# GpSimd's low-part subtractions of the expert weights, one instruction of 1024 columns against four of 256

## The chip, the cores and the metric

The kernel is one program on one core of a Trainium2 chip. The metric is the device time of one execution in microseconds (us). A core has a TensorE for matmuls (PE; PEld is its weight load), a VectorE (DVE), a ScalarE (ACT), a GpSimd (POOL), a SyncE (SP) that issues transfers, and 16 DMA engines. Each engine works through its own list of instructions in order and meets the others only at semaphores.

## The reference

It is one layer of a hybrid streaming encoder over 1024 prompt frames and 64 frames of a running stream, 1088 tokens of width 1024. After a mixer (band attention and retention) comes the part that the change touches, a retrieval over 16384 experts of one neuron each:

```python
qry = (hb @ w_query).reshape(t, P_HEADS, 2, P_HALF)
...
expert = jnp.take_along_axis(cand_i, best_pos, axis=-1)      # 8 heads x 16 experts a token
gate = jax.nn.softmax(best_s, axis=-1)
a = jnp.einsum('td,thkd->thk', hb, expert_u[expert]).astype(jnp.float32)
act = (jax.nn.gelu(a, approximate=False) * gate).astype(hb.dtype)
return jnp.einsum('thk,thkd->td', act, expert_v[expert])
```

Everything is in fp32. A matmul of fp32 precision is made of three passes over numbers split into a high part (rounded to fp32r) and a low part (the rest): high times high, high times low, low times high.

## The kernel before, in words

The program runs five stages one after the other: projection, mixer (`mix_...`), routing, spreading of the gates, and the experts (`exp_...`), which begin near 1900 us and take the second half of the time. The expert stage does its work in two ways at once.

**The dense way**, for the last 704 tokens: all 16384 experts are computed, 128 at a time, in 128 steps j. Step j needs `u_raw` and `v_raw` of j (128x1024 each, a transfer of 512 KB each, from SP), split in two parts. ScalarE copies them to fp32r (`u_hi`, `v_hi`), GpSimd subtracts that from the raw values (`u_lo`, `v_lo`, line 1587 and line 1592). TensorE multiplies `u` with the hidden state (`up`, L1800), ScalarE applies gelu (`ge`), VectorE multiplies by the gates (`pr`, L1703), ScalarE rounds it (`am_hi`), VectorE subtracts (`am_lo`, L1708), TensorE multiplies with `v` (`vp`, L1813), and VectorE adds the result from PSUM to `acc` (L1715). A step has 96 matmuls of 352 columns.

**The gathered way**, for the first 384 tokens: each of the 128 experts of a token is fetched by its index. A fetch is an indirect DMA that GpSimd issues (L1601): it brings one row of 1024 for each of 128 tokens into one of four slots of `ring`. VectorE then does a "pick" over the slot: in the first half of the stage a multiply with reduction into `dot` (L1722, followed by a short read of the accumulator), in the second half a multiply-add into `own` (L1728). There are 768 fetches and 768 picks, 12 in a pair of steps.

The order on each engine is written out by hand. For each pair of steps, q, VectorE goes through 16 places m: an addition at each, a product (L1703) at m = 0, 4, 8 and 12, an `am_lo` (L1708) at m = 1, 5, 9 and 13, and a pick at 12 of them:

```python
LATE = (3, 4, 6, 7, 8, 9, 10, 11, 12, 13, 14, 15)
SPOTS = (0, 1, 2, 3, 4, 6, 7, 8, 10, 11, 12, 14)
```

GpSimd goes through the same pair as four splits with three fetches behind each: `split_u`, three fetches, `split_v`, three fetches, `split_u`, three fetches, `split_v`, three fetches. Fetch n waits until pick n-4 has left its slot (`after(pool, taken, n - RING + 1)`), pick n waits until fetch n has landed (`row_in`). TensorE alternates blocks of six `up` and six `vp` matmuls; at m = 0 and m = 8 its `vp` part waits for an `am_lo`, and each `vp` block waits until VectorE has emptied one of four PSUM banks (`added`).

Of the kernel before, what the change touches and what calls it, by code (L numbers as in the profile page):

```python
# [8 lines left out]
F32 = mybir.dt.float32  # L9
# [3 lines left out]
ALU = mybir.AluOpType  # L13
# [4 lines left out]
D = 1024  # L18
# [35 lines left out]
def after(eng, sem, value):  # L54

    if not isinstance(value, int) or value > 0:
        eng.wait_ge(sem, value)
# [1427 lines left out]
def experts(nc, d):  # L1485
# [11 lines left out]
    with Stage(nc, "exp") as s:  # L1497
        h2 = [s.sb("h2_hi", [P, KD, TD], F32R), s.sb("h2_lo", [P, KD, TD], F32R)]
        acc = s.sb("acc", [P, KD, TD])
        u_raw = s.sb("u_raw", [P, 2, KD * P])  # L1500
        v_raw = s.sb("v_raw", [P, 2, D])
        u = [s.sb("u_hi", [P, 2, KD * P], F32R), s.sb("u_lo", [P, 2, KD * P], F32R)]
        v = [s.sb("v_hi", [P, 4, D], F32R), s.sb("v_lo", [P, 4, D], F32R)]
# [77 lines left out]

        @block.gpsimd
        def _(pool):

            def split_u(j):
                pool.wait_ge(u_hi_ready, j + 1)
                nc.gpsimd.tensor_tensor(u[1][:, j % 2, :], u_raw[:, j % 2, :], u[0][:, j % 2, :].bitcast(F32),  # L1587
                                        ALU.subtract).then_inc(u_lo_ready, 1)

            def split_v(j):  # L1590
                pool.wait_ge(v_hi_ready, j + 1)
                nc.gpsimd.tensor_tensor(v[1][:, j % 4, :], v_raw[:, j % 2, :], v[0][:, j % 4, :].bitcast(F32),  # L1592
                                        ALU.subtract).then_inc(v_lo_ready, 1)

            def fetch(n):

                if n >= 2 * PICKS:
                    return
                after(pool, taken, n - RING + 1)
                k, t = n % PICKS // NS, n % NS  # L1600
                nc.gpsimd.indirect_dma_start(  # L1601
                    out=ring[:, n % RING, :], out_offset=None, in_=d["u_rows"] if n < PICKS else d["v"],
                    in_offset=bass.IndirectOffsetOnAxis(ap=eid[:, t, k:k + 1], axis=0)).then_inc(row_in[n % RING], 16)

            pool.wait_ge(eid_in, 16)
            for n in range(RING):
                fetch(n)
            split_u(0)
            for q in range(NQ):
                n = EACH * q + RING  # L1610
                split_u(2 * q + 1)
                for s_ in range(0, 3):
                    fetch(n + s_)
                split_v(2 * q)
                for s_ in range(3, 6):
                    fetch(n + s_)
                if q + 1 < NQ:
                    split_u(2 * q + 2)
                for s_ in range(6, 9):
                    fetch(n + s_)  # L1620
                split_v(2 * q + 1)
                for s_ in range(9, EACH):
                    fetch(n + s_)
# [280 lines left out]
```

## Time and profile before

| | |
|---|---|
| median of 3 runs | 4056.29 us (4054.91 to 4061.13) |
| the profiled execution: time / span | 4058.68 us / 4056.7 us |
| PE busy | 3551.1 us, 88% |
| DVE busy | 3035.6 us, 75% |
| POOL busy | 1640.1 us, 40% |
| ACT busy | 1109.6 us, 27% |
| mean granted TensorE clock | 0.955 |

The busy time of an engine is what lies between the starts and the ends of its instructions. An instruction that has started and is held up before it can read its data counts as busy. So the mean duration of a kind of instruction is to be compared with its shortest one.

### The profile page before, as it was taken

The page shows a single profiled execution, that of the slowest core. Times are in us where ns is not written, and L with a number is a line of the kernel's source. Part 1 is how long each engine was busy: PE and PEld are TensorE (multiplying, and loading weights), DVE is VectorE, ACT ScalarE, POOL GpSimd, SP SyncE. Part 2 cuts the span into 40 slices and gives each one's busy share as a digit, 9 for nine tenths or more (in the row PEclk, how much of TensorE's full clock was granted, in tenths as well). Part 3 has the DMA queues.
Part 4 walks back from the last instruction along what each step waited for, and adds up shares of the span by engine and source line. Part 5 has one row for each costly group of instructions (what it writes and reads, how often), then busy time and mean ns, then how long its engine had stood idle before and what let it go on. Part 6 is the DMA issues. An engine that isn't in the chain of part 4 may idle for free.

```text
span 4056.7 us, 55884 instructions
## 1 busy us (share of the span) xinstructions
PE 3551.1 (88%) x20014; PEld 3207.7 (79%) x20014; DVE 3035.6 (75%) x5650; ACT 1109.6 (27%) x1636; POOL 1640.1 (40%) x1154
## 2 busy tenths in 40 slices
PE   7999978999979842663899999999999999999998
PEld 6888865566568732663899999999999999999998
DVE  3110104433337998995999999999999999999998
ACT  3211213333211113994222222222222222222221
POOL 0000013232000000001766666666667777777774
PEclk9999988999989976997999999999999999999999
DMA  3222233222230000557888888888878888888887
GB/s 128 96 94 92 88 137 145 97 85 90 65 131 24 4 7 16 166 166 228 283 275 273 280 274 278 279 276 273 278 262 273 281 283 279 277 281 277 282 281 244
DMA packets 335784, 775.24 MB, mean 191 GB/s; under 512 B 39088, under 2 KB 142512, under 8 KB 334256
## 3 DMA queue, kind: packets, MB, share of 16 engines
q0 software_dynamic: 110592, 402.70, 29.5%
q1 hardware_dynamic: 198160, 336.04, 24.7%
q10 hardware_dynamic: 26912, 35.13, 2.4%
q8 instruction: 46, 0.75, 0.1%
q14 instruction: 74, 0.61, 0.0%
HBM read 680.73 MB, written 93.06 MB: 191 GB/s over the span
## 4 chain that ended last, share of the span: by engine, by line
DVE 37%; issue 9%; PE 5%; DMA 1%; POOL 1%; DVEq 0%; ACTq 0%; ACT 0%
DVE exp_ring L1722 11%; DVE exp_acc L1715 10%; DVE exp_pr L1703 9%; DVE exp_own L1728 5%; PE exp_vp L1813 3%; PE exp_up L1800 2%; DVE exp_am_lo L1708 2%; DMA exp_acc<-scratch_h2T 1%; POOL exp_ring L1601 0%; DVE exp_dot L1722 0%; DMA exp_ring<-in_v,exp_eid 0%; DMA exp_ring<-in_u_rows,exp_eid 0%; DMA exp_u_raw<-scratch_x 0%; DMA out_yp<-exp_u_raw 0%; POOL exp_v_lo L1592 0%
## 5 line engine op out<-in xcount | busy, mean ns | idle before, releaser
L1813 PE MATMUL exp_vp<-exp_am_hi,exp_v_hi 128*128 128x352 f32 x2048 | 672.9, 329 | 105.4 <-DVE exp_am_lo L1708 99.7
L1800 PE MATMUL exp_up<-exp_h_hi,exp_u_hi 128*128 128x352 f32 x2048 | 667.0, 326 | 56.0 <-POOL exp_u_lo L1587 56.0
L1800 PE MATMUL exp_up<-exp_h_lo,exp_u_hi 128*128 128x352 f32 x2048 | 666.6, 325 | 0.0
L1813 PE MATMUL exp_vp<-exp_am_lo,exp_v_hi 128*128 128x352 f32 x2048 | 666.1, 325 | 0.0
L1800 PE MATMUL exp_up<-exp_h_hi,exp_u_lo 128*128 128x352 f32 x2048 | 665.9, 325 | 0.0
L1813 PE MATMUL exp_vp<-exp_am_hi,exp_v_lo 128*128 128x352 f32 x2048 | 665.5, 325 | 0.0
L1728 DVE SCALAR_TENSOR_TENSOR exp_own<-exp_ring,exp_dot,exp_own 128x1024 f32<-128x1024 f32 x381 | 663.6, 1742 | 2.0 <-DMA exp_ring<-in_v,exp_eid 2.0
L1601 POOL DMA_INDIRECT exp_ring<-in_u_rows,exp_eid x384 | 379.6, 989 | 667.4 <-DVE exp_dot L1722 328.9
L1722 DVE CUSTOM_DVE_ANT_0 exp_ring<-exp_ring,exp_own 128x1024 f32<-128x1024 f32 x384 | 546.5, 1424 | 5.5 <-DMA exp_ring<-in_u_rows,exp_eid 5.4
L1601 POOL DMA_INDIRECT exp_ring<-in_v,exp_eid x384 | 421.8, 1098 | 269.0 <-DVE exp_own L1728 219.7
L1715 DVE TENSOR_TENSOR exp_acc<-exp_acc,exp_vp 128x352 f32<-128x352 f32 x1024 | 520.4, 509 | 6.3 <-PE exp_vp L1813 6.3
L1652 ACT CAST exp_am_hi<-exp_pr 128x352 fp32r<-128x352 f32 x256 | 124.8, 487 | 1353.3 <-DVE exp_pr L1703 1328.9
L1813 PEld LDWEIGHTS exp_vp<-exp_am_hi,exp_v_hi 128*128 128x128 f32 x2048 | 390.0, 190 | 123.4 <-DVE exp_acc L1715 106.3
L1800 PEld LDWEIGHTS exp_up<-exp_h_hi,exp_u_hi 128*128 128x128 f32 x2048 | 390.7, 191 | 56.5 <-DMA exp_ident<-in_ident 53.8
L1703 DVE TENSOR_TENSOR exp_pr<-exp_ge,exp_gt 128x352 f32<-128x352 f32 x256 | 397.3, 1552 | 0.5 <-ACT exp_ge L1647 0.5
L1800 PEld LDWEIGHTS exp_up<-exp_h_hi,exp_u_lo 128*128 128x128 f32 x2048 | 391.1, 191 | 0.0
L1800 PEld LDWEIGHTS exp_up<-exp_h_lo,exp_u_hi 128*128 128x128 f32 x2048 | 390.8, 191 | 0.0
L1813 PEld LDWEIGHTS exp_vp<-exp_am_lo,exp_v_hi 128*128 128x128 f32 x2048 | 390.4, 191 | 0.0
L1813 PEld LDWEIGHTS exp_vp<-exp_am_hi,exp_v_lo 128*128 128x128 f32 x2048 | 390.3, 191 | 0.0
L1592 POOL TENSOR_TENSOR exp_v_lo<-exp_v_raw,exp_v_hi 128x1024 fp32r<-128x1024 f32 x128 | 360.8, 2819 | 2.8
L249 DVE TENSOR_TENSOR prj_w_lo<-prj_w_raw,prj_w_hi 128x1024 fp32r<-128x1024 f32 x44 | 52.1, 1222 | 401.4 <-ACT prj_w_hi L184 401.3
L1587 POOL TENSOR_TENSOR exp_u_lo<-exp_u_raw,exp_u_hi 128x1024 fp32r<-128x1024 f32 x128 | 322.1, 2517 | 19.0 <-ACT exp_u_hi L1637 16.6
(201 smaller groups left out, 5598.6 us busy)
## 6 DMA issues: line engine op xcount, KB each, us to landing
exp_u_raw<-in_u SPq DMA_DIRECT2D x128, 512.0 KB, 5.4
exp_v_raw<-in_v SPq DMA_DIRECT2D x128, 512.0 KB, 3.7
exp_gt<-scratch_gates SPq DMA_DIRECT2D x128, 352.0 KB, 4.6
scratch_gates<-spr_g SPq DMA_DIRECT2D x5, 8192.0 KB, 30.6
scratch_z<-prj_zo ACTq DMA_DIRECT2D x33, 768.0 KB, 3.5
prj_w_raw<-in_w_in SPq DMA_DIRECT2D x44, 512.0 KB, 4.6
mix_zg<-scratch_z SPq DMA_DIRECT2D x9, 1024.0 KB, 5.3
rt_wq<-in_w_q SPq DMA_DIRECT2D x4, 2048.0 KB, 17.9
```

The lines of the kernel that those rows point to most:

```text
L249: V.tensor_tensor(w_lo[:, slot, 2 * c:2 * c + 2, :], w_raw[:, c % 2, :, :], w_hi[:, slot, 2 * c:2 * c + 2, :].bitcast(F32), ALU.subtract). ...
L1587: nc.gpsimd.tensor_tensor(u[1][:, j % 2, :], u_raw[:, j % 2, :], u[0][:, j % 2, :].bitcast(F32), ALU.subtract).then_inc(u_lo_ready, 1)
L1592: nc.gpsimd.tensor_tensor(v[1][:, j % 4, :], v_raw[:, j % 2, :], v[0][:, j % 4, :].bitcast(F32), ALU.subtract).then_inc(v_lo_ready, 1)
L1601: nc.gpsimd.indirect_dma_start(out=ring[:, n % RING, :], out_offset=None, in_=d["u_rows"] if n < PICKS else d["v"], in_offset=bass.Indirec ...
L1652: nc.scalar.copy(am[0][:, half, o, cols(g)], pr[:, g, :]).then_inc(am_hi_ready, 1)
L1703: V.tensor_tensor(pr[:, g, :], ge[:, g, :], gt[:, j % 2, cols(g)], ALU.mult).then_inc(prod_ready, 1)
L1708: V.tensor_tensor(am[1][:, half, o, cols(g)], pr[:, g, :], am[0][:, half, o, cols(g)].bitcast(F32), ALU.subtract).then_inc(am_lo_ready, 1)
L1715: V.tensor_tensor(acc[:, k, cols(g)], acc[:, k, cols(g)], vp[:, n % 4, 0:GW], ALU.add).then_inc(added, 1)
L1722: V.tensor_tensor_reduce(out=ring[:, r, :], in0=ring[:, r, :], in1=own[:, t, :], scale=1.0, scalar=0.0, op0=ALU.mult, op1=ALU.add, accum_o ...
L1728: V.scalar_tensor_tensor(out=own[:, t, :], in0=ring[:, r, :], scalar=dot[:, t, k:k + 1], in1=own[:, t, :], op0=ALU.mult, op1=ALU.add).then ...
L1800: last = nc.tensor.matmul(up[:, 2 * o + g, 0:GW], u[a][:, o, k * P:(k + 1) * P], h2[b][:, k, cols(g)], start=(k == 0 and n == 0), stop=(k ...
L1813: last = nc.tensor.matmul(vp[:, m % 4, 0:GW], v[a][:, 2 * (1 - half) + o, k * P:(k + 1) * P], am[b][:, 1 - half, o, cols(g)], start=(o == ...
```

## The change

Both subtractions of GpSimd in the expert stage, `split_u` and `split_v`, are issued as four instructions over 256 columns each, in place of one over 1024. The wait ahead of them stays ahead of the first quarter, and the semaphore that tells the others is raised by the fourth. The values are the same.

```diff
@@ experts, @block.gpsimd
+            quarters = [slice(c * D // 4, (c + 1) * D // 4) for c in range(4)]
 
             def split_u(j):
                 pool.wait_ge(u_hi_ready, j + 1)
-                nc.gpsimd.tensor_tensor(u[1][:, j % 2, :], u_raw[:, j % 2, :], u[0][:, j % 2, :].bitcast(F32),
-                                        ALU.subtract).then_inc(u_lo_ready, 1)
+                for c in quarters:
+                    last = nc.gpsimd.tensor_tensor(u[1][:, j % 2, c], u_raw[:, j % 2, c], u[0][:, j % 2, c].bitcast(F32),
+                                                   ALU.subtract)
+                last.then_inc(u_lo_ready, 1)
 
             def split_v(j):
                 pool.wait_ge(v_hi_ready, j + 1)
-                nc.gpsimd.tensor_tensor(v[1][:, j % 4, :], v_raw[:, j % 2, :], v[0][:, j % 4, :].bitcast(F32),
-                                        ALU.subtract).then_inc(v_lo_ready, 1)
+                for c in quarters:
+                    last = nc.gpsimd.tensor_tensor(v[1][:, j % 4, c], v_raw[:, j % 2, c], v[0][:, j % 4, c].bitcast(F32),
+                                                   ALU.subtract)
+                last.then_inc(v_lo_ready, 1)
```

GpSimd's list at the start of the expert stage, before: the first four fetches, the splits of u for steps 0 and 1, and then three fetches behind each split (a row stands for as many instructions as its x says).

```order
L1601 DMA exp_ring<-in_u_rows,exp_eid 128x1024 x4
L1587 TENSOR_TENSOR exp_u_lo<-exp_u_raw,exp_u_hi 128x1024 x2
L1601 DMA exp_ring<-in_u_rows,exp_eid 128x1024 x3
L1592 TENSOR_TENSOR exp_v_lo<-exp_v_raw,exp_v_hi 128x1024
L1601 DMA exp_ring<-in_u_rows,exp_eid 128x1024 x3
L1587 TENSOR_TENSOR exp_u_lo<-exp_u_raw,exp_u_hi 128x1024
L1601 DMA exp_ring<-in_u_rows,exp_eid 128x1024 x3
```

The same place of the changed kernel, whose lines are numbered a little higher:

```order
L1606 DMA exp_ring<-in_u_rows,exp_eid 128x1024 x4
L1589 TENSOR_TENSOR exp_u_lo<-exp_u_raw,exp_u_hi 128x256 x8
L1606 DMA exp_ring<-in_u_rows,exp_eid 128x1024 x3
L1596 TENSOR_TENSOR exp_v_lo<-exp_v_raw,exp_v_hi 128x256 x4
L1606 DMA exp_ring<-in_u_rows,exp_eid 128x1024 x3
L1589 TENSOR_TENSOR exp_u_lo<-exp_u_raw,exp_u_hi 128x256 x4
L1606 DMA exp_ring<-in_u_rows,exp_eid 128x1024 x3
```

Nothing has moved past anything else: where one subtraction stood, four stand, and the fetches keep their places between the splits. The lists of the other engines are unchanged.

## Rows read from the trace of the kernel before

**Rows 1.** Busy time by engine in two stretches of the expert stage, one in each half

```profile
2300.00:2600.00 300.00, 285.70 (x1748) 283.14 (x1747) 300.00 (x438) 68.23 (x111) 198.55 (x147) 0.98 0.82 275
3200.00:3500.00 300.00, 287.89 (x1761) 285.03 (x1759) 300.00 (x332) 69.45 (x111) 224.68 (x147) 0.98 0.82 279
```

**Rows 2.** Waits, 2000 to 4056 us: engine, line, waited for, us, times, longest

```profile
POOL exp_ring L1601 <- DVE exp_dot L1722: 312.9, 263, 3.0
POOL exp_ring L1601 <- DVE exp_own L1728: 219.7, 216, 1.6
...
PE exp_vp L1813 <- DVE exp_am_lo L1708: 90.6, 55, 2.7
```

**Rows 3.** Timeline of PE, first half of the stage (start us, duration us)

```profile
2700.00 0.32 PE L1813 MATMUL exp_vp<-exp_am_hi,exp_v_lo 128*128 128x352 f32 x1
...
2701.90 0.32 PE L1813 MATMUL exp_vp<-exp_am_hi,exp_v_lo 128*128 128x352 f32 x1
```

**Rows 4.** Groups by line, 2100 to 4000 us: count, busy us, mean ns, idle before

```profile
L1728 DVE SCALAR_TENSOR_TENSOR exp_own<-exp_ring,exp_dot,exp_own 128x1024 f32<-128x1024 f32 x372 | 648.7, 1744 | 2.0 <-DMA exp_ring<-in_v,exp_eid 2.0
...
L1722 DVE CUSTOM_DVE_ANT_0 exp_ring<-exp_ring,exp_own 128x1024 f32<-128x1024 f32 x317 | 449.0, 1416 | 0.0
...
L1703 DVE TENSOR_TENSOR exp_pr<-exp_ge,exp_gt 128x352 f32<-128x352 f32 x231 | 355.8, 1540 | 0.5 <-ACT exp_ge L1647 0.5
...
L1592 POOL TENSOR_TENSOR exp_v_lo<-exp_v_raw,exp_v_hi 128x1024 fp32r<-128x1024 f32 x115 | 326.2, 2837 | 2.4
```

**Rows 5.** Timeline of POOL, two splits apart, first half of the stage

```profile
2717.70 0.94 POOL L1601 DMA_INDIRECT exp_ring<-in_u_rows,exp_eid  x1 [0.64 <-DVE exp_dot L1722]
2718.66 2.60 POOL L1592 TENSOR_TENSOR exp_v_lo<-exp_v_raw,exp_v_hi 128x1024 fp32r<-128x1024 f32 x1
2721.41 1.07 POOL L1601 DMA_INDIRECT exp_ring<-in_u_rows,exp_eid  x1
...
2735.12 2.59 POOL L1592 TENSOR_TENSOR exp_v_lo<-exp_v_raw,exp_v_hi 128x1024 fp32r<-128x1024 f32 x1
```

**Rows 6.** Timeline of DVE around the first of those splits

```profile
2717.78 1.22 DVE L1722 CUSTOM_DVE_ANT_0 exp_ring<-exp_ring,exp_own 128x1024 f32<-128x1024 f32 x1
...
2718.93 2.71 DVE L1703 TENSOR_TENSOR exp_pr<-exp_ge,exp_gt 128x352 f32<-128x352 f32 x1
2721.56 0.51 DVE L1715 TENSOR_TENSOR exp_acc<-exp_acc,exp_vp 128x352 f32<-128x352 f32 x1
2721.99 1.21 DVE L1722 CUSTOM_DVE_ANT_0 exp_ring<-exp_ring,exp_own 128x1024 f32<-128x1024 f32 x1
```

**Rows 7.** Timeline of POOL in the mixer stage, rotary of one tile

```profile
629.50 1.26 POOL L549 TENSOR_TENSOR mix_rot<-mix_part 128x512 f32<-128x512 f32 x1
630.84 2.12 POOL L546 TENSOR_TENSOR mix_part<-mix_zqk,mix_cs 128x512 f32<-128x512 f32 x1
632.92 2.25 POOL L547 TENSOR_TENSOR mix_part<-mix_zqk,mix_cs 128x512 f32<-128x512 f32 x1
```

**Rows 8.** Timeline of DVE at the same time, mixer stage

```profile
630.22 1.62 DVE L701 TENSOR_TENSOR mix_qk<-mix_za,mix_qk_rs 128x1024 f32<-128x1024 f32 x1
631.87 2.17 DVE L707 TENSOR_TENSOR mix_qk<-mix_qk,mix_g_qk 128x1024 f32<-128x1024 f32 x1
```

**Rows 9.** Timeline of POOL around a split, second half of the stage

```profile
3152.81 3.10 POOL L1592 TENSOR_TENSOR exp_v_lo<-exp_v_raw,exp_v_hi 128x1024 fp32r<-128x1024 f32 x1
3156.06 1.76 POOL L1601 DMA_INDIRECT exp_ring<-in_v,exp_eid  x1 [0.16 <-issue]
3158.13 0.94 POOL L1601 DMA_INDIRECT exp_ring<-in_v,exp_eid  x1 [0.30 <-issue]
```

**Rows 10.** Timeline of DVE at the same time, second half of the stage

```profile
3153.99 3.00 DVE L1728 SCALAR_TENSOR_TENSOR exp_own<-exp_ring,exp_dot,exp_own 128x1024 f32<-128x1024 f32 x1
...
3158.21 1.27 DVE L1728 SCALAR_TENSOR_TENSOR exp_own<-exp_ring,exp_dot,exp_own 128x1024 f32<-128x1024 f32 x1
```

**Rows 11.** DMA issues, 2100 to 2900 us: count, median us from issue to landing

```profile
exp_ring<-in_u_rows,exp_eid POOLq DMA_INDIRECT x291, 5.2
```

## The prediction

> **What bounds the kernel now.** I read the busy time by stretch first, to see which engines are full in the expert stage, then the waits, then the groups by line, then the timelines of GpSimd and VectorE side by side.
>
> In both halves of the stage VectorE is busy for all of the 300 us, TensorE for 286 and 288, GpSimd for 199 and 225 [rows 1]. TensorE is not the bound, though nearly: two of its matmuls that are twelve apart start 1.90 us apart, 0.158 us each [rows 3], so the 192 of a pair of steps take 30.4 us, and a pair lasts 32.9 us (two splits of v two places apart start 16.46 us apart, two splits and their fetches being half a pair [rows 5]). The missing 2.5 us is TensorE's wait for `am_lo`, 90.6 us in 55 waits [rows 2], and what follows it.
>
> VectorE's own work is much less than its busy time. A pick takes 1.15 us of its time (2717.78 to 2718.93), an operation over 352 columns 0.43 to 0.44 (2721.56 to 2721.99) [rows 6]. A pair has 12 picks and 24 of the others (16 additions, 4 products, 4 `am_lo`): 13.8 + 10.4 = 24.2 us of 32.9. The rest is in stretched instructions. The product has a mean of 1.54 us against 0.51, the pick of the first half 1.42 against 1.21, that of the second 1.74 against 1.27 [rows 4, 6, 10]; the additions, one of whose inputs is in PSUM, are not stretched. In the window of the groups this is 238 + 65 + 175 = 478 us for twice 115 splits, 2.1 us a split.
>
> The timelines show why. The split of v starts at 2718.66 and ends at 2721.26; the product that starts at 2718.93 ends at 2721.64, 0.38 us after it [rows 5, 6]. In the second half the split ends at 3155.91 and a pick that began at 3153.99 ends at 3156.99, 1.08 us after [rows 9, 10]. So a VectorE instruction with two SBUF inputs and a GpSimd subtraction do not read at the same time; the one that comes second stands until the other has ended. I call what they share the port. It is what lets TensorE wait: VectorE stands four times in a pair, and its `am_lo` comes late.
>
> **The change, part by part.** Nothing is moved between engines and no wait is added; four instructions stand for one, 256 times.
>
> *What a quarter takes.* The expert stage has no subtraction of this size, the mixer has ones of 512 columns. Alone they take 1.26 us. The one that starts at 632.92 finds the port taken by a VectorE instruction that ends at 634.04, and ends at 635.17, 1.13 us later; its predecessor ends 1.12 us after VectorE's at 631.84 [rows 7, 8]. So 0.13 us pass before the port is needed, and reading takes 1.13/512 = 2.2 ns a column: 0.57 us a quarter. The next instruction starts 0.04 us before the former ends (632.92 against 632.96). Four quarters with nobody in between take 0.13 + 4 x 0.565 + 3 x 0.09 = 2.66 us, where one instruction takes 2.39 us alone (2.60 from 2718.66, less the 0.21 us between its 0.13 and the end of the pick at 2719.00 [rows 5, 6]). That is +0.27 us a split. A split has no cheaper bound than 0, and 0.27 is the direct estimate. The Trainium skill (GPSIMD Engine Reference, Instruction dispatch) puts the cost of one more instruction at one indirect call, tens of cycles; by that three more would cost about 0.1 us as an estimate, and the sum below would be 0.17 us a split lower.
>
> *Who gets the port between two quarters.* In the mixer two GpSimd instructions follow each other at 632.96 with no wait between them, and VectorE's, which stood since 631.87, reads between them: it ends at 634.04, and only then does the second read [rows 7, 8]. So a waiting VectorE instruction gets in at each boundary, and the next quarter waits for all of it.
>
> *What VectorE gains.* Its product now stands for at most one quarter, 0.57 us, not 2.2. Behind the product comes an addition, which needs no port, and the second quarter reads under it; then a pick gets in, and so on. I take 0.8 us of standing a split in place of 2.1. VectorE would need 24.2 + 4 x 0.8 = 27.4 us a pair, under TensorE's 30.4. On this side alone the stage would fall to TensorE's rate.
>
> *What GpSimd loses.* Quarters two to four each wait for an instruction that has got in: a product (0.37 us of port), a pick (1.07, its 1.21 less 0.14), then an `am_lo` (0.37) or a second pick. That is 1.8 to 2.5 us. The gaps of 0.09 lie inside these waits. A split then takes 2.4 + 1.8 = 4.2 to 4.9 us, against 2.60 and 3.10 now [rows 5, 9].
>
> *What hangs behind it.* GpSimd is in order, and three fetches are queued behind each split. A fetch takes 0.94 us, and one right behind another starts 0.31 us after it (3157.82 to 3158.13) [rows 9]. A split and its fetches now take 8.23 us (16.46/2), and GpSimd has 533 us of waiting for picks in some 250 of these cycles, 2.1 us each [rows 2]; about 0.3 of each wait is there in any case, so its slack is near 1.5 us. With the change a cycle takes at least 4.2 + 0.15 + 3 x 0.94 + 2 x 0.31 = 7.8 us, and with the longer split 8.5. To this comes that a fetch can be held at the port as well: the one at 3156.06 takes 1.76 us, since a pick reads until 3156.99 [rows 9, 10]. Now most fetches start right after a pick has ended and meet none; one that is late starts at any time and loses up to 0.82. With one such a cycle takes 8.6 to 9.3 us.
>
> *What VectorE then waits for.* There are four slots. A fetch lands 5.2 us after its issue [rows 11]. The fetch behind a split can go when the split is done; the pick that frees its slot ends some 0.3 us after the split's start. From that pick's end to the landing now pass 2.6 - 0.3 + 0.15 + 5.2 = 7.6 us, after the change 9.3 to 9.9. At 30.4 us a pair a pick comes every 2.53 us, and the row must be there 4 x 2.53 - 1.2 = 8.9 us after; at today's 32.9, 9.8. So the four slots carry neither the longer split at TensorE's rate, nor surely at today's. The standing at the port, which hid nothing, is exchanged for waiting for rows, and `am_lo` is as late as before.
>
> *The sum.* GpSimd's cycle becomes the length of a quarter of a pair. Its bounds are 7.8 us (no fetch held, shortest split) and 9.3 (a fetch held in each, longest split). The bounds are far apart and no row decides between them; I take the middle, 8.55, since GpSimd's lateness partly heals itself: while VectorE waits for a row, quarters run back to back in 2.66 us. Against 8.23 that is +0.32 us in each of some 250 cycles, +80 us. The profiled execution took 4058.7 us, so 4139, and that execution lies 2.4 us above the median: 4137. The bounds give 4058.7 - 0.43 x 250 = 3951 and 4058.7 + 1.07 x 250 = 4326.
>
> **The rivals.**
>
> *Faster: the fetches keep up.* If splits stay near 4.2 us and no fetch is held, the cycle is 7.8 us and the time about 3950. It cannot be under TensorE's 30.4 us a pair: 4058.7 - 2.5 x 63 = 3901. For it speaks that VectorE really needs only 27.4 us, and that GpSimd has slack. Against it speak the fetch of 1.76 us [rows 9] and the four slots. It decides at a mean split and its fetches of 8.23 us. A rule of the Trainium skill (SBUF — State Buffer, Who interferes with whom) would have it so: VectorE instructions with two SBUF inputs are said to hold up only those of GpSimd that read SBUF, and descriptor generation is said to need the write interface; then no fetch would be held. The fetch that ends 0.83 us after a pick's end, in place of 0.94 after its own start, says otherwise here. Chance 0.25.
>
> *GpSimd keeps the port over its four quarters.* Then VectorE stands for 2.66 us in place of 2.39 and gains nothing: +0.27 x 250 = +67 us, 4124. The mixer's rows speak against it, though these are instructions of another kind on VectorE's side. Chance 0.08.
>
> *Far slower.* Each quarter waits for a full pick, fetches are held more than once: 9.3 us a cycle, 4326. For it speaks that picks are half of VectorE's time; against it that a VectorE which waits for rows holds nobody up. Chance 0.12.
>
> *No difference.* Gain and loss cancel within 8 us, or another wait sets the pace. Chance 0.05.
>
> **How the numbers follow.** The forecast, slower by tens of us through late rows, has 0.50 and gives 4137. A measurement of this kernel can tell about 0.2%, 8 us. Slower by more: 0.50 + 0.08 + 0.12 = 0.70; within: 0.05; faster: 0.25. The range 3985 to 4250 takes in the forecast, the second and fourth rivals, half of the faster rival (whose own numbers run from 3901 to 4048) and half of the far slower one: 0.50 + 0.08 + 0.05 + 0.12 + 0.06 = 0.81. The likeliest case alone runs from 4065 to 4220, a cycle of 8.26 to 8.88 us.
>
> **What the profile after would show.** (1) Product: mean under 1.1 us, where it is 1.54. (2) Quarters: shortest near 0.70, mean 1.0 to 1.2, four together over 4 us. (3) VectorE's waits for `exp_ring`, next to nothing now (2.0 us of idle time ahead of L1728 [rows 4]), at 300 us or more. (4) GpSimd's waits for picks well under 533 us. (5) TensorE's waits as long as before or longer. The prediction is wrong if VectorE finds its rows landed (then faster), if four quarters take 2.7 us and the product is as long as now (then the port is kept), or if the DMA engines, busy for 0.82 now [rows 1], set the pace.

## The result, and the profile after

| | before | after |
|---|---|---|
| median | 4056.26 us (4 runs) | 4201.06 us (4 runs, 4196.15 to 4203.23) |
| ratio, 95% interval | | 1.0353 [1.0335, 1.0371] |
| span of the profiled execution | 4056.7 us | 4200.9 us |
| mean granted TensorE clock | 0.955 | 0.941 |

The change makes the kernel 145 us slower. The busy time in the same two stretches as [rows 1] (columns: the stretch, its length, busy time and instructions of PE, PEld, DVE, ACT, POOL, the granted clock, the DMA share, GB/s):

```profile
2300.00:2600.00 300.00, 278.04 (x1649) 275.46 (x1648) 247.34 (x412) 63.89 (x102) 267.87 (x241) 0.95 0.77 261
3200.00:3500.00 300.00, 273.99 (x1627) 270.84 (x1626) 243.81 (x306) 64.67 (x103) 258.24 (x238) 0.95 0.75 257
```

VectorE was busy for all of the 300 us and is now idle for 53 and 56 of them. GpSimd went from 199 and 225 us to 268 and 258. TensorE issued 1649 matmuls in place of 1748: that is the slowdown. Its mean granted clock fell from 0.98 to 0.95, of which more below. The groups by line of the kernel after, 2100 to 4000 us, which answer to [rows 4]:

```profile
L1733 DVE SCALAR_TENSOR_TENSOR exp_own<-exp_ring,exp_dot,exp_own 128x1024 f32<-128x1024 f32 x323 | 471.6, 1460 | 145.8 <-DMA exp_ring<-in_v,exp_eid 144.4 <-issue 0.6
L1596 POOL TENSOR_TENSOR exp_v_lo<-exp_v_raw,exp_v_hi 128x256 fp32r<-128x256 f32 x432 | 471.1, 1121 | 1.9
L1727 DVE CUSTOM_DVE_ANT_0 exp_ring<-exp_ring,exp_own 128x1024 f32<-128x1024 f32 x322 | 462.4, 1436 | 128.7 <-DMA exp_ring<-in_u_rows,exp_eid 126.8 <-issue 1.2
...
L1589 POOL TENSOR_TENSOR exp_u_lo<-exp_u_raw,exp_u_hi 128x256 fp32r<-128x256 f32 x432 | 407.2, 973 | 1.9
L1606 POOL DMA_INDIRECT exp_ring<-in_u_rows,exp_eid x318 | 393.8, 1238 | 104.7 <-issue 65.1 <-DVE exp_dot L1727 36.6
...
L1708 DVE TENSOR_TENSOR exp_pr<-exp_ge,exp_gt 128x352 f32<-128x352 f32 x216 | 152.6, 707 | 0.5 <-ACT exp_ge L1652 0.5
```

The product fell from a mean of 1540 ns to 707. Ahead of the picks (L1733, L1727) stand 146 and 129 us of idle time for rows that have not landed, where [rows 4] had 2.0 and 0.0. A quarter takes 973 and 1121 ns, a fetch of the first half 1238. The waits of the same kernel, 2000 to 4200 us (us in total, times, longest), beside [rows 2]:

```profile
DVE exp_own L1733 <- DMA exp_ring<-in_v,exp_eid: 170.6, 109, 7.1
POOL exp_ring L1606 <- issue: 147.7, 577, 1.0
DVE exp_ring L1727 <- DMA exp_ring<-in_u_rows,exp_eid: 136.6, 109, 5.9
PE exp_vp L1818 <- POOL exp_v_lo L1596: 131.4, 49, 6.2
...
POOL exp_ring L1606 <- DVE exp_own L1733: 66.0, 69, 2.2
POOL exp_ring L1606 <- DVE exp_dot L1727: 39.2, 47, 2.2
PE exp_vp L1818 <- DVE exp_am_lo L1713: 35.3, 12, 4.7
```

GpSimd's waits for picks fell from 533 us to 105. Both other engines now wait for GpSimd: VectorE for its rows (307 us), TensorE for its `exp_v_lo` (131 us), which it waited for once in the kernel before, for 4.6 us. The page's chain that ended last says the same; "POOL" is its first entry:

```profile
POOL 28%; DMA 12%; DVE 8%; issue 5%; PE 2%; ACTq 0%; DVEq 0%; ACT 0%
```

One split in detail. The timeline of POOL in the kernel after (start us, duration us), the kind of place that [rows 5] showed:

```profile
2729.96 0.94 POOL L1606 DMA_INDIRECT exp_ring<-in_u_rows,exp_eid  x1 [1.40 <-DVE exp_dot L1727]
2730.92 4.59 POOL L1596 TENSOR_TENSOR exp_v_lo<-exp_v_raw,exp_v_hi 128x256 fp32r<-128x256 f32 x4
2735.66 1.77 POOL L1606 DMA_INDIRECT exp_ring<-in_u_rows,exp_eid  x1
2737.73 1.25 POOL L1606 DMA_INDIRECT exp_ring<-in_u_rows,exp_eid  x1 [0.30 <-issue]
```

The timeline of DVE at the same time:

```profile
2731.18 1.06 DVE L1708 TENSOR_TENSOR exp_pr<-exp_ge,exp_gt 128x352 f32<-128x352 f32 x1
2732.16 0.51 DVE L1720 TENSOR_TENSOR exp_acc<-exp_acc,exp_vp 128x352 f32<-128x352 f32 x1
2732.59 1.33 DVE L1727 CUSTOM_DVE_ANT_0 exp_ring<-exp_ring,exp_own 128x1024 f32<-128x1024 f32 x1
...
2734.29 0.62 DVE L1713 TENSOR_TENSOR exp_am_lo<-exp_pr,exp_am_hi 128x352 fp32r<-128x352 f32 x1
...
2735.26 1.33 DVE L1727 CUSTOM_DVE_ANT_0 exp_ring<-exp_ring,exp_own 128x1024 f32<-128x1024 f32 x1
```

The quarters start at 2730.92, 2731.82, 2732.80 and 2734.48. VectorE's product, a pick and an `am_lo` each get their turn in the 4.59 us; none stands for more than 0.55 us. A second pick gets in behind the last quarter, reads until 2736.59, and the fetch that starts at 2735.66 ends only at 2737.43, after 1.77 us. In the kernel after, 40% of the fetches take over 1.2 us, in the kernel before 10%, and each of these has a pick beside it, behind whose end it ends by 0.83 us in the median.

The Trainium skill (SBUF — State Buffer, Who interferes with whom) says that a VectorE instruction with two SBUF inputs contends with a GpSimd instruction that reads SBUF and not with one that only writes it, and infers that descriptor generation needs the write interface. By that this fetch would not be held; the trace disagrees, with 1.77 us against 0.94. A fetch here takes its indices from a tile in SBUF (`exp_eid`); which of its accesses is held, no run shows.

TensorE pays for its waits a second time, in its clock. The timeline of PE in the kernel after, around one such wait:

```profile
2299.66 0.42 PE L1818 MATMUL exp_vp<-exp_am_hi,exp_v_hi 128*128 128x352 f32 x1 [3.08 <-POOL exp_v_lo L1596]
2299.92 0.32 PE L1818 MATMUL exp_vp<-exp_am_lo,exp_v_hi 128*128 128x352 f32 x1
2300.08 0.32 PE L1818 MATMUL exp_vp<-exp_am_hi,exp_v_lo 128*128 128x352 f32 x1
...
2300.99 0.50 PE L1805 MATMUL exp_up<-exp_h_lo,exp_u_hi 128*128 128x352 f32 x1
2301.28 0.50 PE L1805 MATMUL exp_up<-exp_h_hi,exp_u_lo 128*128 128x352 f32 x1
```

After 3.08 us without work two matmuls start 0.16 us apart, at 2.4 GHz, and 1 us later 0.29 us apart, at a granted clock of 0.5, which is 1.2 GHz. Over the expert stage TensorE's clock was at 1.2 GHz for 75 us in the kernel before and for 208 in the kernel after. From the first matmul of the stage to the last, 2125 us became 2274; of the 149 us, 94 are idle time of TensorE and 55 are busy time, the same matmuls at the lower clock. Each of its 42 falls between 2000 and 4180 us of the kernel after comes in a wait of TensorE or shortly behind one, so the lower clock follows from the waits, for the low part of `v` above all. How much of the loss would be left without it was not tested.

### The profile page after: what moved, and what is told of

It is laid out like the page before. It is cut to its first block, busy times and chain, and to the rows that moved or that the text cites. A ratio compares the mean times of both kernels' runs of the same rounds, so it can differ in the third digit from the quotient of the medians.

```text
span 4200.9 us, 56652 instructions
## 1 busy us (share of the span) xinstructions
PE 3604.4 (86%) x20014; PEld 3256.3 (78%) x20014; DVE 2773.9 (66%) x5650; ACT 1112.1 (26%) x1636; POOL 2124.9 (51%) x1922
## 4 chain that ended last, share of the span: by engine, by line
POOL 28%; DMA 12%; DVE 8%; issue 5%; PE 2%; ACTq 0%; DVEq 0%; ACT 0%
POOL exp_ring L1606 11%; POOL exp_v_lo L1596 11%; POOL exp_u_lo L1589 6%; DMA exp_ring<-in_v,exp_eid 6%; DMA exp_ring<-in_u_rows,exp_eid 6%; DVE exp_ring L1727 3%; DVE exp_own L1733 2%; PE exp_vp L1818 2%; DVE exp_acc L1720 1%; PE exp_up L1805 1%; DMA exp_acc<-scratch_h2T 1%; DVE exp_am_lo L1713 0%; DVE exp_pr L1708 0%; DMA exp_u_raw<-scratch_x 0%; DVE exp_acc L1699 0%
## 5 line engine op out<-in xcount | busy, mean ns | idle before, releaser
L1818 PE MATMUL exp_vp<-exp_am_hi,exp_v_hi 128*128 128x352 f32 x2048 | 689.4, 337 | 196.4 <-POOL exp_v_lo L1596 133.9
L1606 POOL DMA_INDIRECT exp_ring<-in_u_rows,exp_eid x384 | 477.3, 1243 | 446.7 <-DMA exp_eid<-scratch_eid 317.4
L1818 PE MATMUL exp_vp<-exp_am_lo,exp_v_hi 128*128 128x352 f32 x2048 | 679.9, 332 | 0.0
L1818 PE MATMUL exp_vp<-exp_am_hi,exp_v_lo 128*128 128x352 f32 x2048 | 677.8, 331 | 0.0
L1733 DVE SCALAR_TENSOR_TENSOR exp_own<-exp_ring,exp_dot,exp_own 128x1024 f32<-128x1024 f32 x381 | 557.4, 1463 | 172.2 <-DMA exp_ring<-in_v,exp_eid 170.6
L1727 DVE CUSTOM_DVE_ANT_0 exp_ring<-exp_ring,exp_own 128x1024 f32<-128x1024 f32 x384 | 553.1, 1441 | 158.6 <-DMA exp_ring<-in_u_rows,exp_eid 156.7
L1596 POOL TENSOR_TENSOR exp_v_lo<-exp_v_raw,exp_v_hi 128x256 fp32r<-128x256 f32 x512 | 555.9, 1117 | 2.2
L1606 POOL DMA_INDIRECT exp_ring<-in_v,exp_eid x384 | 457.5, 1191 | 149.5 <-issue 75.4
L1589 POOL TENSOR_TENSOR exp_u_lo<-exp_u_raw,exp_u_hi 128x256 fp32r<-128x256 f32 x512 | 478.6, 966 | 18.3 <-ACT exp_u_hi L1642 16.2
L1818 PEld LDWEIGHTS exp_vp<-exp_am_hi,exp_v_lo 128*128 128x128 f32 x2048 | 401.4, 196 | 0.0
L292 PE MATMUL prj_zp<-prj_w_hi,prj_hT_hi 128*128 128x512 f32 x792 | 310.0, 391 | 4.4 <-DVE prj_w_lo L249 4.4
```

The costliest lines, as they stand in the source:

```text
L292: last = nc.tensor.matmul(zp[:, bank(i), :], hT[p][:, k, i * P:(i + 1) * P], (w_hi, w_lo)[q][:, slot, k, :], start=(k == 0 and n == 0), st ...
L1589: last = nc.gpsimd.tensor_tensor(u[1][:, j % 2, c], u_raw[:, j % 2, c], u[0][:, j % 2, c].bitcast(F32), ALU.subtract)
L1596: last = nc.gpsimd.tensor_tensor(v[1][:, j % 4, c], v_raw[:, j % 2, c], v[0][:, j % 4, c].bitcast(F32), ALU.subtract)
L1606: nc.gpsimd.indirect_dma_start(out=ring[:, n % RING, :], out_offset=None, in_=d["u_rows"] if n < PICKS else d["v"], in_offset=bass.Indirec ...
L1727: V.tensor_tensor_reduce(out=ring[:, r, :], in0=ring[:, r, :], in1=own[:, t, :], scale=1.0, scalar=0.0, op0=ALU.mult, op1=ALU.add, accum_o ...
L1733: V.scalar_tensor_tensor(out=own[:, t, :], in0=ring[:, r, :], scalar=dot[:, t, k:k + 1], in1=own[:, t, :], op0=ALU.mult, op1=ALU.add).then ...
```

## The experiments

For each kernel four numbers were taken from the trace, all between 2100 and 3850 us or from pairs 5 to 55. "Split" is from the start of its first piece to the end of its last, mean. "Fetch" is the mean duration of the issue. "Stood" is what VectorE's products, `am_lo` and picks took beyond their shortest, for each split and its three fetches. "Cycle" is the time from one split to the next; the stage has 256 of them. In e3 the split has a fetch inside it.

| kernel | pieces of a split | time us | ratio to before | split | fetch | stood | cycle |
|---|---|---|---|---|---|---|---|
| before | 1 | 4056 | | 2.67 | 1.04 | 2.12 | 8.24 |
| e8_v_halves | u 1, v 2 | 4032.9 | 0.9948 [0.9932, 0.9965] | u 2.46, v 3.30 | 1.11 | 1.89 | 8.12 |
| e1_halves | 2 | 4022.7 | 0.9912 [0.9895, 0.9928] | 2.98 | 1.15 | 1.86 | 8.09 |
| e7_thirds | 3 | 4117.8 | 1.0157 [1.0140, 1.0174] | 3.34 | 1.16 | 1.62 | 8.38 |
| after | 4 | 4201.1 | 1.0353 [1.0335, 1.0371] | 4.04 | 1.22 | 0.96 | 8.81 |
| e11_sixths | 6 | 4356.1 (one run) | | 4.71 | 1.18 | 0.70 | 9.41 |
| e2_eighths | 8 | 4296.3 | 1.0590 [1.0573, 1.0608] | 4.64 | 1.22 | 1.72 | 9.16 |
| e3_between | 4 | 4299.1 | 1.0594 [1.0577, 1.0612] | 5.79 | 1.31 | 1.37 | 9.19 |
| e4_ring5 | 4 | 4203.4 | 1.0358 [1.0341, 1.0375] | 3.98 | 1.26 | 1.16 | 8.80 |
| e5_onein_quarters | 4 | 3916.1 | 0.9651 [0.9634, 0.9667] | 3.02 | 1.00 | 0.68 | 7.67 |
| e6_onein_whole | 1 | 3944.8 | 0.9719 [0.9703, 0.9736] | 2.41 | 0.98 | 1.63 | 7.78 |
| e9_vector_both | none | 3916.7 | 0.9655 [0.9641, 0.9668] | none | 1.08 | 0.03 | 7.68 |
| e10_vector_u_halves_v | v 2 | 3960.6 | 0.9764 [0.9749, 0.9779] | v 3.05 | 1.07 | 0.94 | 7.82 |

The theory, as on record: VectorE gets in between the pieces, so it stands less and GpSimd's split grows; GpSimd is in order, its fetches come late, and GpSimd's cycle sets the pace. First rival: the loss is the fixed cost of more instructions. Second rival: the rows are late because of four slots and the landing time.

### e1_halves: two pieces of 512

```diff
-                for c in quarters:
+                for c in [slice(0, 512), slice(512, 1024)]:
```

> Two instructions of 512 columns a split. Theory (GpSimd's in-order queue is what the change overloads: at each boundary a VectorE instruction gets the port and the rest of the split and the three fetches behind it wait): one boundary in place of three, a split of 2.8 to 3.5 us, a cycle of split and three fetches of 7.2 to 7.8 us where 8.8 is measured after the change, so GpSimd keeps up, VectorE stands about 1.3 us a split in place of 2.1, and the time is 3940 to 4030 us, faster than the kernel before. Rival (each further instruction costs a fixed amount: 144 us over 768 more instructions is 0.19 us each): 4056 + 256 x 0.19 = 4104 us.

4022.7 us: faster than both kernels, by 0.9% against before. The rival by which the time grows with each instruction falls: with one more a split the kernel gains 35 us (4058.0 is the median of before in the same comparison). The timelines of POOL and of DVE of this kernel around one split:

```profile
2701.49 3.03 POOL L1588 TENSOR_TENSOR exp_u_lo<-exp_u_raw,exp_u_hi 128x512 fp32r<-128x512 f32 x2
2704.68 1.76 POOL L1605 DMA_INDIRECT exp_ring<-in_u_rows,exp_eid  x1 [0.15 <-issue]
```

```profile
2701.76 1.60 DVE L1707 TENSOR_TENSOR exp_pr<-exp_ge,exp_gt 128x352 f32<-128x352 f32 x1
...
2703.72 1.88 DVE L1726 CUSTOM_DVE_ANT_0 exp_ring<-exp_ring,exp_own 128x1024 f32<-128x1024 f32 x1
```

The product stands through the first half only and reads between the two. But the pick behind it now meets the second half and stands 0.67 us. So VectorE's standing fell only from 2.12 to 1.86 us a cycle, where I had reckoned with 1.3, and in this kernel it is divided otherwise: 111 us in products where it was 227, 122 in picks of the first half where it was 65. GpSimd still waits for picks (154 and 142 us of waits), so it is not the bound: what VectorE gains is kept. The stage is 33 us shorter by TensorE's account, 13 of them less idle time and 20 less busy time: its clock was at 1.2 GHz for 34 us of the stage in place of 75. So more than half of what TensorE gained here is its clock, beside waits for `am_lo` that are shorter in sum (78 us, where they were 91).

### e8_v_halves and e7_thirds: where it turns

```diff
-                for c in quarters:
+                for c in [slice(0, 352), slice(352, 688), slice(688, 1024)]:
```

That is e7, in both splits. In e8 `split_v` has the two halves of e1 and `split_u` one instruction, as before.

> Halves for v alone, u whole. Theory: each split in halves gives VectorE back part of its standing while GpSimd keeps up, so about half of the gain of halves for both: 4030 to 4050 us. If the low part of v is what TensorE waits for once splits are long, keeping v whole and not u would be the better choice, and this run is no faster than the kernel before.

> Three instructions a split (352, 336 and 336 columns). Two boundaries, a split between the 2.98 us of halves and the 4.04 us of quarters, near 3.5 us; with 0.15, three fetches of 1.2 and two gaps of 0.3 a cycle of GpSimd's own time of 7.9 us, just under the 8.23 us of the kernel before. Theory: 4030 to 4110 us, between halves and quarters. If only the number of boundaries counted linearly from the kernel before, halves could not have been faster, so this run places the turn.

Half of the edit of e1 gives 4032.9, as expected: 24 us of the 35. Three pieces give 4117.8, 8 us above the expected stretch. The turn lies between two and three pieces. Between those two kernels VectorE's standing falls by 0.24 us a cycle and the split grows by 0.36; VectorE waits 78 us for rows ahead of its multiply-add with three pieces (21 us in e1, 22 in e8).

### e2_eighths and e11_sixths: more pieces

```diff
-                for c in quarters:
+                for c in [slice(0, 128), slice(128, 256), slice(256, 384), slice(384, 512), slice(512, 640), slice(640, 768), slice(768, 896), slice(896, 1024)]:
```

e11 has 176, 176 and four times 168 columns.

> Eight instructions of 128 columns a split. Theory of the overloaded queue: VectorE stands for at most 0.28 us at a time but gets in at seven boundaries, a split gets longer than with quarters (mean 4.0 us), cycle 9.3 to 10 us, time 4300 to 4450 us. Rival of a fixed cost for each instruction: 4056 + 1792 x 0.19 = 4393 us, with splits that get longer by 0.19 us a piece whether VectorE reads or not. This run alone does not tell the two apart by its time; the mean of a piece that meets no VectorE instruction does: near 0.41 us by the first (0.13 and 128 columns of 2.2 ns), 0.6 by the second.

> Six instructions a split (176 and 168 columns). With pieces of 256 columns VectorE got in at each boundary, with 128 only ahead of the last piece in most splits. If the size of a piece decides, 168 columns lie between: pieces that are held in positions 2 to 5 are common if VectorE can still get in, rare if not. Time by the overloaded queue: 4250 to 4350 us.

Eight pieces give 4296, just under the expected stretch, and six give 4356 in a single run, just above theirs: six are no better than eight. A piece of 128 columns that meets nobody takes 0.46 us, nearer the 0.41 of the theory than the 0.6 of the rival. But VectorE does not get in at seven boundaries, as the timelines of POOL and of DVE of e2 show:

```profile
2709.49 4.34 POOL L1595 TENSOR_TENSOR exp_v_lo<-exp_v_raw,exp_v_hi 128x128 fp32r<-128x128 f32 x8
2713.99 1.25 POOL L1605 DMA_INDIRECT exp_ring<-in_u_rows,exp_eid  x1 [0.16 <-issue]
```

```profile
2709.58 3.94 DVE L1726 CUSTOM_DVE_ANT_0 exp_ring<-exp_ring,exp_own 128x1024 f32<-128x1024 f32 x1
```

The pick stands 2.7 us, over seven pieces, and gets in only ahead of the eighth. Counted over the 256 splits of the trace, a piece of 128 columns that is held (over 0.65 us, where one alone takes 0.46) is the eighth in 240 of them and each of the second to seventh in 2 to 40. In e11, with 168 columns, the second to the sixth are held in 117, 85, 95, 119 and 137 of 256; in the kernel after the second to fourth in 128, 149 and 159. A boundary at which nothing is held may be one at which nobody waits, so these counts don't tell how often a waiting instruction is passed over. Counted from VectorE's side between 2100 and 3850 us, by the product, `am_lo` or pick that begins to stand during the first piece: with quarters 84 of 94 read behind that piece and 9 behind all four; with halves 128 of 171 and 43; with thirds 88 of 130 and 42; with eighths 2 of 41, and 39 waited over seven pieces. So passing over is the rule at 128 columns and happens at all sizes. It is not the size alone: in e5, whose picks read one SBUF input (below), 53 of the 229 products stand over all four quarters, for 2.1 us. One of them, in the timelines of DVE and of POOL of e5:

```profile
2116.93 2.60 DVE L1709 TENSOR_TENSOR exp_pr<-exp_ge,exp_gt 128x352 f32<-128x352 f32 x1
```

```profile
2116.32 2.82 POOL L1590 TENSOR_TENSOR exp_u_lo<-exp_u_raw,exp_u_hi 128x256 fp32r<-128x256 f32 x4
```

Of these 53 products 51 begin with under 0.2 us left of the first quarter; of the 109 that read behind the first quarter, one does. In e7 the passed-over picks begin at any time of a piece, so this is not the whole rule either. Why an instruction is passed over was not tried further.

Alone, eight pieces would take 3.4 us and six 3.1, reckoned from 0.46 and 0.54 us a piece; of the 4.64 and 4.71 us measured, 1.2 and 1.6 are time held. With eight GpSimd waits 13 us for picks in the whole stage: its own work is the cycle. With six it waits over 100 us and the cycle is longer still; why is not shown.

### e3_between: a fetch between two halves of the split

```diff
-                split_u(2 * q + 1)
-                for s_ in range(0, 3):
-                    fetch(n + s_)
...
+                    if j < PK:
+                        split(j, (0, 1))
+                    fetch(n + s_)
+                    if j < PK:
+                        split(j, (2, 3))
+                    fetch(n + s_ + 1)
+                    fetch(n + s_ + 2)
```

> Quarters as in the change, but the first of the three fetches of a cycle is issued after the second quarter. If the loss is GpSimd's total time (theory), the fetch comes sooner but the low part of v later, and the time stays at 4150 to 4260 us. If the loss is only that a fetch behind a long split lands late (rival), this takes most of it away: 4000 to 4080 us.

4299.1: the rival falls as far as this run can tell, and the theory's range (to 4260) is missed as well. The edit also puts a fetch ahead of the second half of each split. The wait of that kernel which stands out, 2000 to 4300 us:

```profile
PE exp_vp L1819 <- POOL exp_v_lo L1601: 234.8, 61, 8.9
```

A fetch between the quarters can wait for its pick, and with it the low part of v. TensorE then stands up to 8.9 us for it. The order by which the split comes ahead of all three fetches is worth keeping.

### e4_ring5: five slots in place of four, on the kernel after

```diff
-    RING = 4
+    RING = 5
```

> Quarters as in the change, with five slots for the fetched rows in place of four; each fetch is released by the pick at the same place and has one pick (2.7 us) more to land. Theory (GpSimd's total time is the bound): within 30 us of the changed kernel, 4170 to 4210 us, VectorE still waits for rows. Rival (the landing time of a late fetch is the bound): at most 4080 us and VectorE's waits for rows gone.

4203.4, against 4201.1: no difference. VectorE still waits for rows, 237 us where it was 307, 2000 to 4300 us:

```profile
DVE exp_own L1733 <- DMA exp_ring<-in_v,exp_eid: 133.8, 74, 6.7
...
DVE exp_ring L1727 <- DMA exp_ring<-in_u_rows,exp_eid: 103.6, 63, 7.9
```

With one more slot every row could be asked for one pick (2.5 us or more) earlier, if GpSimd had the time. It mostly has not: it waits 83 us for these picks in place of 105. The rows are issued late, and the second rival falls: the slot took 70 us off VectorE's waits and nothing off the time.

### e5_onein_quarters and e6_onein_whole: picks with one SBUF input

```diff
-                    V.tensor_tensor_reduce(out=ring[:, r, :], in0=ring[:, r, :], in1=own[:, t, :], scale=1.0, scalar=0.0,
-                                           op0=ALU.mult, op1=ALU.add, accum_out=dot[:, t, k:k + 1]).then_inc(taken, 1)
+                    V.tensor_scalar(ring[:, r, :], ring[:, r, :], 1.0, None, ALU.mult, ALU.add,
+                                    accum_out=dot[:, t, k:k + 1]).then_inc(taken, 1)
...
-                    V.scalar_tensor_tensor(out=own[:, t, :], in0=ring[:, r, :], scalar=dot[:, t, k:k + 1], in1=own[:, t, :],
-                                           op0=ALU.mult, op1=ALU.add).then_inc(taken, 1)
+                    V.tensor_scalar(own[:, t, :], ring[:, r, :], dot[:, t, k:k + 1], None, ALU.mult, ALU.add,
+                                    accum_out=spare[:, t:t + 1]).then_inc(taken, 1)
```

The same edit on the kernel after (e5) and on the kernel before (e6). Both leave out the product with the hidden row and the sum over the experts, so they are for their times only.

> Quarters as in the change, with picks that read one SBUF input (a multiply by a scalar with an accumulator) in place of two; the product with the hidden row and the sum over the experts of a token are left out. Theory (what makes splits and fetches long is that picks take the port between them): a split 2.8 to 3.2 us, fetches 0.94 us each, a cycle of some 6.6 us of GpSimd's time, so TensorE's rate is reached: 3900 to 3970 us. Rival (768 more instructions cost their time whoever reads beside them): 4150 us or more.

> The kernel before with the same picks of one SBUF input, the same work left out. Theory: VectorE stands only with its product or its low-part subtraction, and the time is 3900 to 3990 us, within 40 us of the same picks with quarters. If picks of this form do share the port, it stays near 4056 us.

3916.1 with quarters, 3944.8 with whole subtractions: the change of this study, which costs 145 us with the real picks, now gains 29 us. GpSimd has the same list as in the kernels with real picks; what has changed is that a pick no longer gets in between its instructions. No other run speaks as plainly for the theory. A stretch of e5 and its groups, 2100 to 3850 us:

```profile
2300.00:2600.00 300.00, 300.00 (x1882) 300.00 (x1881) 269.23 (x471) 73.82 (x117) 234.28 (x276) 1.00 0.85 299
```

```profile
L1607 POOL DMA_INDIRECT exp_ring<-in_v,exp_eid x376 | 379.4, 1009 | 201.9 <-DVE exp_own L1734 138.7 <-issue 53.2 <-DVE exp_own L1731 8.5
L1597 POOL TENSOR_TENSOR exp_v_lo<-exp_v_raw,exp_v_hi 128x256 fp32r<-128x256 f32 x456 | 362.5, 825 | 2.2
...
L1709 DVE TENSOR_TENSOR exp_pr<-exp_ge,exp_gt 128x352 f32<-128x352 f32 x229 | 265.1, 1158 | 0.2 <-ACT exp_ge L1653 0.2
```

The groups of e6, same window:

```profile
L1704 DVE TENSOR_TENSOR exp_pr<-exp_ge,exp_gt 128x352 f32<-128x352 f32 x225 | 438.1, 1947 | 0.5 <-ACT exp_ge L1648 0.5
...
L1593 POOL TENSOR_TENSOR exp_v_lo<-exp_v_raw,exp_v_hi 128x1024 fp32r<-128x1024 f32 x112 | 269.6, 2407 | 2.3
```

With such picks the fetches fall back to a mean of 0.98 to 1.00 us and the whole split to 2.41, what it takes alone. The product of e6 stands 1.4 us (1947 ns against 510) and delays TensorE; with quarters it stands less and TensorE is busy for all of the 300 us, at a granted clock of 1.00. The two effects of the picks on GpSimd, the stretched split and the held fetches, went away together here; they were not taken apart. A fixed cost is there as well: three further instructions take GpSimd 0.43 us a split (below), of the 1.37 by which its mean grew from before to after, and the three fetches grew by 0.54. Here, where GpSimd has time to spare, those 0.43 us cost nothing; in the kernel after it has little.

### e9_vector_both and e10_vector_u_halves_v: the subtractions on VectorE

```diff
@@ VectorE, at the 16 places of a pair; GpSimd's own split_u and split_v go
+                    if m == 2:
+                        split_u(2 * q + 1)
+                    elif m == 9 and q + 1 < NQ:
+                        split_u(2 * q + 2)
+                    if m == 5:
+                        split_v(2 * q)
+                    elif m == 12:
+                        split_v(2 * q + 1)
```

e10 moves the two of u only, and leaves v to GpSimd in two pieces of 512.

> The low parts of u and v are subtracted on VectorE, one instruction of 1024 columns each, four in a pair of steps at places m = 2, 5, 9 and 12; GpSimd only issues the fetches. Theory: VectorE stands 2.1 us for each split on GpSimd, and would take about 1.15 us to do it itself; its own work is 24.2 + 4 x 1.15 = 28.8 us a pair, under TensorE's 30.4, nobody else asks for the port but the fetches, so 3900 to 3960 us. Rival: VectorE is the full engine (busy for all of the time before) and more work on it makes it slower: 24.2 plus 4.6 plus its waits for ScalarE's high parts, 4060 us or more.

> The low part of u on VectorE, that of v on GpSimd in two halves. VectorE: 24.2 + 2 x 1.15 + 2 x about 1.5 of standing = 29.5 us a pair, near TensorE's 30.4: 3910 to 3990 us, at or a little above the run with both on VectorE.

Both came out as expected: 3916.7 and 3960.6. e9 is the fastest kernel of the study with the whole computation, 3.45% under the kernel before and 6.7% under the kernel after (0.9655/1.0353 = 0.9326). The two stretches of e9, and its groups from 2100 to 3850 us:

```profile
2300.00:2600.00 300.00, 300.00 (x1882) 300.00 (x1881) 284.66 (x509) 74.68 (x118) 126.15 (x118) 1.00 0.87 299
3200.00:3500.00 300.00, 300.00 (x1883) 300.00 (x1881) 288.31 (x392) 75.06 (x119) 126.15 (x117) 1.00 0.87 298
```

```profile
L1707 DVE TENSOR_TENSOR exp_u_lo<-exp_u_raw,exp_u_hi 128x1024 fp32r<-128x1024 f32 x114 | 138.7, 1217 | 0.0
L1712 DVE TENSOR_TENSOR exp_v_lo<-exp_v_raw,exp_v_hi 128x1024 fp32r<-128x1024 f32 x114 | 138.7, 1217 | 0.0
L1697 DVE TENSOR_TENSOR exp_pr<-exp_ge,exp_gt 128x352 f32<-128x352 f32 x228 | 117.9, 517 | 0.2 <-ACT exp_ge L1641 0.2
```

A subtraction that cost GpSimd 2.4 us and VectorE 2.1 us of standing costs VectorE 1.22 us of its own. The product is back at 517 ns. TensorE is busy throughout, at a granted clock of 1.00 where it was 0.98, and its cycle of 7.68 us is near the 7.6 (30.4/4) that the prediction named as its floor. VectorE has 4 to 5% left.

## Why the prediction was right, and where its terms were off

The direction, the mechanism and the range held. The forecast of 4137 us was 64 us low; 4201 lies inside the range of 3985 to 4250 and inside the likeliest case's own 4065 to 4220. Its steps in order:

**What a quarter takes: mis-sized.** One quarter alone takes 0.74 us and the next follows 0.70 us after its start, so four take 0.74 + 3 x 0.70 = 2.84 us, +0.43 a split over the 2.41 of one instruction, 0.14 for each further instruction. The prediction had 2.66 and +0.27. Alone, pieces of 1024, 512, 336, 256, 168 and 128 columns take 2.40, 1.30, 0.92, 0.74, 0.54 and 0.46 us: 0.18 us and 2.17 ns a column. The reading was right, the fixed part (0.13 taken from the mixer) too small. The estimate from the Trainium skill (GPSIMD Engine Reference, Instruction dispatch), some 0.1 us for the three, is further off; +0.43 was measured.

**Who gets the port, and what VectorE gains: right for most, not for all.** The second to fourth quarters are held in 128, 149 and 159 of 256 splits. "Gets in at each boundary", drawn from one pair of instructions of the mixer, was too strong: of 94 instructions that began to stand in the first quarter, 84 got in behind it and 9 stood over all four. VectorE stood 0.96 us a cycle, where 0.8 was said.

**What GpSimd loses: right in kind, too large.** A split takes 4.04 us in the mean, under the 4.2 to 4.9 of the prediction. A VectorE that waits for rows, or is in an addition, holds nobody.

**What hangs behind it: the term that was too small.** The fetches take 1.22 us in the mean, 3 x (1.22 - 0.94) = 0.84 us held in a cycle. The middle value of 8.55, with the middle split of 4.55, had left 8.55 - 4.55 - 0.15 - 2.82 - 0.62 = 0.41 for them. The cycle was reckoned without any wait for picks; 105 us in some 250 cycles, 0.42 each, remained. Put together: -0.51 for the split, +0.43 for the fetches, +0.42 for the waits, so 8.55 + 0.34 = 8.89, where 8.81 was measured. And 8.81 - 8.24 = 0.57 us in each of 252 cycles is 144 us, the whole of the loss. The middle came out 64 us low because two terms were low and one was high. That it came so near is in part luck: errors of 0.4 to 0.5 us in three terms partly cancelled, and the middle of two bounds was itself a choice that no row supported.

**What VectorE then waits for: the waits right, a cause wrong.** It waits 307 us for rows, as said. But the four slots are not what costs the time: with five it is the same, though the waits for rows are 70 us shorter. The rows are issued late because GpSimd has little time to spare.

**TensorE.** Its waits within `vp` went from 91 us to 183 (131.4 for `exp_v_lo`, 35.3 for `am_lo`, 16.6 for `acc`). That they would be longer was right; that it would be `am_lo` again was not. A longer split delays its own result as well, and the prediction did not name that consumer. Nor had it a term for the clock: TensorE spent 208 us of the stage at 1.2 GHz, where it had been 75, and its busy time grew by 55 us. GpSimd's cycle contains that, since it is the cycle of all three engines.

**The rivals.** "GpSimd keeps the port" fell on the product's 707 ns as an account of the whole; it came true in 9 of those 94 cases here, for 53 of 229 products in e5, and, up to the last piece, in most splits of e2. "The fetches keep up" needed a mean cycle under 8.23 us; it is what happens with two pieces (8.09). The rule by which a fetch is not held fell on the fetches of 1.77 us, and on their mean, which follows the picks: 1.22 us with real picks and quarters, 1.00 with picks of one SBUF input.

What stays open: how much of the 0.57 us the held fetches alone are worth, how much the clock adds to it, and what decides whether a standing VectorE instruction gets in at a boundary or is passed over.

## What to carry to other kernels

Cutting an instruction so that another engine gets in between its pieces shortens that engine's stand by making the cut engine's queue longer: before doing it, add up the cut engine's whole cycle, with everything that is queued behind the pieces and can be held in the same way, and look at who waits for the result of the cut instruction. Here two pieces gained 0.9%, three lost 1.6% and four 3.5%. Where two engines stand for each other several times in a step, the better question is whether the work can go to the engine that was standing: the subtraction cost VectorE 1.2 us of work in place of 2.1 us of standing, and gave 3.5%.

## What the runs showed of the hardware

- A standing VectorE instruction mostly gets in at the next boundary between GpSimd subtractions of 256 columns (84 of 94 that began to stand in the first of four), and mostly doesn't at 128 (2 of 41). Once passed over it usually stood to the last piece or to the end: a pick 2.7 us over seven pieces, and, beside picks of one SBUF input, a product 2.1 us over four of 256.
- The issue of an indirect DMA is held by a VectorE pick with two SBUF inputs: 1.76 to 1.77 us in place of 0.94 in the rows shown, its end 0.83 us behind the pick's. With picks of one SBUF input the mean was 0.98 to 1.00.
- A GpSimd subtraction costs 0.18 us beside its 2.17 ns a column, and the next starts 0.04 us before its end (2.40 us for 1024 columns, 0.74 for 256, 0.46 for 128, alone).
- Behind a wait of 3.08 us TensorE's granted clock went from 2.4 to 1.2 GHz, and matmuls of 352 columns started 0.29 us apart in place of 0.16.
